# Trainium2 kernel: output projection, norm and feed-forward of each block in one stage, weights tile by tile, the norm's factor at the exits from PSUM

## The reference, cut to what matters

```python
def _rmsnorm(x, w):
    xf = x.astype(jnp.float32)
    y = xf * lax.rsqrt(jnp.mean(xf * xf, axis=-1, keepdims=True) + EPS)
    return (y * w.astype(jnp.float32)).astype(x.dtype)

def _conv_ffn(h, w_up, ffn_conv, ffn_conv_bias, w_down):
    gate, up = _split(h @ w_up, (D_FF, D_FF))
    gate = _dwconv(gate, ffn_conv) + ffn_conv_bias
    return (jax.nn.silu(gate) * up) @ w_down

for l in range(DEPTH):
    h = _rmsnorm(x, mix_norm[l])
    x = x + _mixer(h, ...)
    h = _rmsnorm(x, ffn_norm[l])
    x = x + _conv_ffn(h, w_up[l], ffn_conv[l], ffn_conv_bias[l], w_down[l])
...
```

## Time and profile before

| | |
|---|---|
| median of 3 runs | 3351.74 us (3351.55 to 3360.6) |
| profiled execution | 3355.1 us, its span 3353.2 us |
| mean granted TensorE clock | 0.962 |
| PE busy | 3059.8 us, 91% |
| PEld / DVE / ACT / POOL busy | 76% / 48% / 35% / 14% |
| DMA | 235 MB, 70 GB/s over the span |

### The profile page before, as it was taken

How to read it: one execution, slowest core, us unless ns; L and a number is a source line. 1 busy time by engine, 2 the same in 40 slices (tenths; PEclk the granted TensorE clock), 3 DMA queues, 4 the chain that set the end, 5 groups by cost and what they waited for, 6 DMA issues and landing times. The chain is left out here.

```text
span 3353.2 us, 40954 instructions
## 1 busy us (share of the span) xinstructions
PE 3059.8 (91%) x15744; PEld 2534.2 (76%) x15744; DVE 1617.2 (48%) x2106; ACT 1181.0 (35%) x1647; POOL 479.8 (14%) x279
## 2 busy tenths in 40 slices
PE   6899899886999989898998978999898999969899
PEld 5799888775887867898887856887676767758787
DVE  4566547533554345565476334553475552233233
ACT  3543543323222234334543232222333652232222
POOL 2332003001000022330030000000162223110000
PEclk9999999998999999999999988999999999989999
DMA  4100300322222231002103222222431222223122
GB/s 148 51 1 1 100 26 20 101 76 78 87 92 72 92 102 49 26 1 75 50 1 101 76 75 88 92 83 82 122 82 49 71 63 79 66 75 98 65 95 93
DMA packets 264333, 235.11 MB, mean 70 GB/s; under 512 B 23188, under 2 KB 247938, under 8 KB 263554
## 3 DMA queue, kind: packets, MB, share of 16 engines
q1 hardware_dynamic: 264194, 233.20, 23.0%
HBM read 226.88 MB, written 6.29 MB: 70 GB/s over the span
## 5 line engine op out<-in xcount | busy, mean ns | idle before, releaser
L120 PE MATMUL PS<-HHI,WHI 128*128 128x512 f32 x2016 | 805.4, 399 | 93.3 <-DVE WLO L172 70.5
L121 PE MATMUL PS<-HLO,WHI 128*128 128x512 f32 x2016 | 797.2, 395 | 0.0
L122 PE MATMUL PS<-HHI,WLO 128*128 128x512 f32 x2016 | 796.6, 395 | 0.0
L172 DVE TENSOR_TENSOR WLO<-RAW,WHI 128x1024 fp32r<-128x1024 f32 (+2 forms) x212 | 361.6, 1707 | 513.8 <-ACT WHI L168 512.7
L168 ACT CAST WHI<-RAW 128x1024 fp32r<-128x1024 f32 (+2 forms) x212 | 304.1, 1437 | 744.3 <-PE PS L122 611.8
L120 PEld LDWEIGHTS PS<-HHI,WHI 128*128 128x128 f32 x2016 | 382.7, 190 | 194.1 <-issue 78.5
L122 PEld LDWEIGHTS PS<-HHI,WLO 128*128 128x128 f32 x2016 | 382.2, 190 | 87.8
L121 PEld LDWEIGHTS PS<-HLO,WHI 128*128 128x128 f32 x2016 | 382.9, 190 | 86.7 <-issue 2.0
L120 PE MATMUL PS<-SH,WHI 128*128 128x512 f32 x800 | 316.9, 396 | 45.1 <-DVE SL L379 45.1
L121 PE MATMUL PS<-SL,WHI 128*128 128x512 f32 x800 | 315.5, 394 | 0.0
L122 PE MATMUL PS<-SH,WLO 128*128 128x512 f32 x800 | 315.5, 394 | 0.0
(11 more groups left out here) (427 smaller groups left out, 4490.6 us busy)
## 6 DMA issues: line engine op xcount, KB each, us to landing
RAW<-in_w_up SPq DMA_DIRECT2D x44, 1024.0 KB, 5.1
RAW<-in_w_in SPq DMA_DIRECT2D x82, 512.0 KB, 4.1
RAW<-in_w_down SPq DMA_DIRECT2D x44, 512.0 KB, 3.3
RAW<-in_w_in SPq DMA_DIRECT2D x20, 1024.0 KB, 5.4
RAW<-in_w_gate SPq DMA_DIRECT2D x32, 512.0 KB, 4.0
RAW<-in_w_mlp SPq DMA_DIRECT2D x16, 1024.0 KB, 5.4
RAW<-in_w_mlp SPq DMA_DIRECT2D x32, 512.0 KB, 3.5
RAW<-in_w_out SPq DMA_DIRECT2D x24, 512.0 KB, 3.5
```

The lines of the kernel that those rows point to most:

```text
L120: e.matmul(out, wh, xh, start=first and n == 0, stop=False)
L121: e.matmul(out, wh, xl, start=False, stop=False)
L122: last = e.matmul(out, wl, xh, start=False, stop=final and n == len(quads) - 1)
L172: self.lo_st.done(dve.tensor_tensor(self.lo[:, s], self.raw[:, s], self.hi[:, s], ALU.subtract), f"unit{s}")
```

## The change

For each of the three blocks the four stages output projection, norm, up projection and down projection become one, `out_and_ffn_stage` (line 1482 of the changed kernel), written out without loops. `rms_stage`, `slab_stage`, `ffn_up_stage`, `mlp_up_stage` and `store_stage` are gone.

- **Weights.** All three projections take weights by output tile: 128 columns of 8 contraction tiles (11 or 8 for the down projection), in rows of 512 bytes. There are four slots instead of two. ACT casts each unit; POOL subtracts each but the first.
- **Output projection.** Per output tile 24 matmuls into one of four banks, then DVE adds it to X (line 1728) and makes XL (line 1713), ACT makes XH = X * weight (line 1673) and the square (line 1676), and PE sums the square two tiles later (line 1593).
- **Norm.** XH and XL hold X times the norm's weight without the factor RS. RS is made by ACT from the sum (lines 1679, 1681), and DVE applies it at the exit from PSUM.
- **Up projection.** The first three tiles are taken together, contraction tile by contraction tile. In a layer DVE does per hidden tile: times RS (line 1740), three taps (1744, 1747), the low part of the hidden tile before (1718), times the up tile (1752), times RS again (1754). ACT does silu (1691) and the high part (1697). In the MLP DVE does relu times RS in one instruction, ACT the square and the high part, DVE the low part.
- **Down projection.** The hidden tiles come in two groups; each group's down projection follows its up projection at once and is added to X. So hidden tiles are kept split, for one group only, in the buffers of M (8 tiles) and of `more`.
- **The stages before.** `branch_stage` and `attention_gate_stage` split M themselves (ACT cast, DVE subtract, one tile later) and load the first two units of w_out.
- **Output.** The transposes of tile m-1 follow tile m of the last down projection; ACT copies them out and SP stores.

```diff
 def branch_stage(...)
+                for r in range(2):
+                    feed.lo_st.wait(sp, T - 1, f"unit{r}")
+                    sp.dma_start(feed.raw[:, r, 0:8, :], k_tiles(w_out)[:, :, r * P:(r + 1) * P]).then_inc(tiles_in[r], 16)
...
+                def mixed_high(t):
+                    act.wait_ge(merged_s, t + 1)
+                    act.copy(MH[:, t, :], M[:, t % 2, :]).then_inc(mh_s, 1)
...
+                def mixed_low(t):
+                    dve.wait_ge(mh_s, t + 1)
+                    dve.tensor_tensor(ML[:, t, :], M[:, t % 2, :], MH[:, t, :], ALU.subtract).then_inc(ml_s, 1)
...
+def out_and_ffn_stage(nc, PS, C, X, mixed, raw01, in01, w_out, norm, w_up, w_down, conv, HID, wide_k, new, out=None):
+    K, N, R3 = X.shape[1], 4, range(3)
+    groups = [range(g * n_hid // 2, (g + 1) * n_hid // 2) for g in range(2)]
+    raw23 = new("RAW", [P, 2, wide_k, P])
+    WHI, WLO = new("WHI", [P, N, wide_k, P], F32R), new("WLO", [P, N, wide_k, P], F32R)
+    XH, XL = split_pair(new)
+    MH, ML = mixed
+    GP, ACC = new("GP", [P, 2, 514]) if conv is not None else None, new("ACC", [P, 2, 512])
...
+            def _(pe):
+                for t in range(K):
+                    low_ready(pe, t)
+                    if t >= 4:
+                        after(pe, dv, f"add{t - 4}")
+                    pt.done(product(pe, PS[:, 3 + t % 4, :], [(*weights(t, k), MH[:, k, :], ML[:, k, :]) for k in range(K)]), f"a{t}")
+                    if t >= 2:
+                        squares(t - 2)
+                for k in range(K):
+                    if k >= K - 1:
+                        squares(K - 2)
+                        squares(K - 1)
+                    after(pe, dv, f"xlo{k}")
+                    for n, tile in enumerate(tiles_in[0:3]):
+                        u = K + n
+                        if k == 0:
+                            low_ready(pe, u)
+                        last = product(pe, tile_bank(tile), [(*weights(u, k), XH[:, k, :], XL[:, k, :])], first=k == 0, final=k == K - 1)
...
+                        if final and m == 0:
+                            after(pe, dv, f"hlo{hidden[-1]}")
+                        elif m == 0:
+                            after(pe, dv, f"hlo{k0 + units[u][0] - 1}")
...
+            def _(act):
+                def high(u):
+                    act.wait_ge(raw_in[u % N], landed[u])
+                    if u >= N:
+                        after(act, pt, jobs[u - N])
+                    ac.done(act.copy(slot(WHI, u), source(u)), f"hi{u}")
...
+                            dv.done(dve.tensor_tensor(gp[:, 1:513], tile_bank((i, 0)), RS[:, :], ALU.mult), f"g{i}")
...
+                            dv.done(dve.tensor_tensor(acc, acc, tile_bank((i, 1)), ALU.mult), f"h{i}")
+                            own(f"h{i}")
+                            dv.done(dve.tensor_tensor(acc, acc, RS[:, :], ALU.mult), f"hr{i}")
...
+            def _(pool):
+                for u in range(1, U):
+                    after(pool, ac, f"hi{u}")
+                    pool.tensor_tensor(slot(WLO, u), source(u), slot(WHI, u), ALU.subtract).then_inc(lo_s, 1)
```

More of the change, by code:

```diff
@@ L262, in _ @@
                     dve.tensor_copy(PAR[:, n:n + m, :].rearrange("p a n -> p (a n)"), PS[:, n // 4, 0:m * P]).then_inc(rows_kept, 1)
[L265 to L319, removed]
@@ L322, in k_tiles @@
 def k_tiles(w):
     return w.rearrange("(k p) n -> p k n", p=P)
[L327 to L399, removed]
-                    if not final:
-                        used.done(last, f"slab{s}")
-                use(0, 0, True, False)
-                use(0, 1, False, False)
-                with pe.Fori(1, K // 2 - 1) as g:
-                    for s in range(2):
-                        use(g, s, False, False)
-                use(K // 2 - 1, 0, False, False)
-                use(K // 2 - 1, 1, False, True)
@@ L1624, in _ @@
             def _(sp):
-                early.load_first(sp)
-                with sp.Fori(1, T) as g:
+                for u in range(2, U):
+                    if u >= N:
+                        low_ready(sp, u - N)
+                    sp.dma_start(source(u), units[u][1]).then_inc(raw_in[u % N], 16)
+                if out is not None:
+                    for m in range(K):
+                        after(sp, ac, f"row{m}")
+                        dst = out.rearrange("(c p) f -> p c f", p=P)[:, :, m * P:(m + 1) * P]
+                        sp.dma_start(dst, ROWS[:, :, m % 2, :]).then_inc(stored[m % 2], 16)
@@ L1627, in _, with weights @@
                     for s in range(2):
[L1628 to L1629 removed]
+                        sp.wait_ge(stored[s], 16 * K // 2)
             @block.tensor
             def _(pe):
[L1633 to L1640 removed]
+                def weights(u, k):
+                    return WHI[:, u % N, k, :], WLO[:, u % N, k, :]
@@ L1672, in _ @@
-                turns(dve, T, body)
-            @block.scalar
-            def _(act):
-                silu.open(act)
-                feed.hi_st.open(act)
-                feed.split_hi(act, 0, 0)
-                feed.split_hi(act, 0, 1)
-                def body(g, more):
-                    for m in range(2):
-                        dve_st.wait(act, g, f"tap2_{m}")
-                        silu.done(act.activation(tile(HID, g * 2 + m), ACC[:, m, :], ACT.Silu), f"tile{m}")
-                        if more:
-                            feed.split_hi(act, g + 1, m)
-                turns(act, T, body)
+                own = lambda name: after(dve, dv, name)
@@ new lines, in _ @@
+                if conv is not None:
+                    dve.memset(GP[:, :, 0:1], 0.0)
+                    dv.done(dve.memset(GP[:, :, 513:514], 0.0), "pad")
+                after(dve, ac, "hi0")
+                dv.done(dve.tensor_tensor(slot(WLO, 0), source(0), slot(WHI, 0), ALU.subtract), "lo0")
+                for t in range(K):
+                    after(dve, pt, f"a{t}")
+                    dv.done(dve.tensor_tensor(X[:, t, :], X[:, t, :], PS[:, 3 + t % 4, :], ALU.add), f"add{t}")
+                    if t:
+                        x_low(t - 1)
```

451 lines of the change are left out of this document (263 added, 188 removed).

## The result

The changed kernel takes 3269.24 us in the median of four executions (3264.25 to 3274.13), the kernel before 3353.85 beside it: a ratio of 0.9745 (95% interval 0.9727 to 0.9763), 84.6 us less. The forecast was 3250 in a range of 3230 to 3290. The profiled execution took 3264.25, where the sum said 3253.2.

What follows compares the result with a forecast made beforehand. PE, busy 3059.8 of 3353.2 us, was taken as the bound, with gains only in its idle time and pace. Layers -63.0 and second block -38.9 made -101.9: 3253.2 profiled, 3250 median, range 3230 to 3290.

Steps and rivals of the forecast that it cites:

- Into the output projection: PE's idle gap before the output projection: 10.15 to 7.3 us, 2.9 gained per layer; 0.8 lost in the second block.
- The norm: Stretch of 34.4 us between output and up projection: only sums stay, 26.0 gained per layer, 26.7 in the second block.
- the stall behind the root: Early up projection: units cast after ACT's root come late, 1.5 us in a layer, 0.8 in the MLP.
- From up to down: PE waits 4.5 us (3.0 to 5.5) before each layer down projection, twice: 4.0 lost; the MLP's 8.90 goes.
- The slow starts: Half clock after PE idles: 2.5 us gained, 1.0 lost per layer; 2.5 and 1.0 gained in the second block.
- PE's pace: Layers' up projection: weights back on multiples of 128 bytes speed up 1056 matmuls, 7.0 us gained per layer.
- the middle, 1.9: M's buffers, 32 bytes short of a multiple, slow 576 matmuls per block: 1.9 us lost, bounds 0 and 3.9.
- The second block: Its terms, from the output projection to the program's end, sum to 38.9 us gained.
- The pace does not come back: Rival, 0.12: WHI's place is not the cause or misplaced M costs as much; 14 us stay out, 3264.
- The norm still stands in the way: Rival, 0.10: ACT and POOL hand over the first three units late, ten us a block, 3280.
- DVE and POOL block one another: Rival, 0.08: in the layers' up projection DVE takes 12.0 us per hidden tile, 1.1 above PE; 3298.
- POOL becomes the bound: Slower-than-before rival, 0.03: POOL's subtraction limits the stages once its mean passes 5.44 us; 3470 at 6.5.

Runs made afterwards that it cites:

- wait_root: Changed kernel, but PE sums the last two squares right behind the output projection and waits for the finished root before the up projection: 3286.82 us, ratio 0.9786.
- late_pool: Changed kernel, but POOL subtracts the two weight units beside a group's last hidden tile only after that tile's low part: 3256.73 us, one execution.
- whi_off: Changed kernel with WHI and WLO of the layers' joint stage moved up 32 bytes, off multiples of 128: 3278.75 us, ratio 0.9767.
- before_gp_pad: Kernel before with 96 bytes of padding behind ACC, so WHI and WLO begin at a multiple of 128 bytes: 3357.38 us, ratio 1.0005.
- m_aligned: Changed kernel with 96 bytes of padding ahead of M's right-hand buffers in each block: 3266.43 us, ratio 0.9725.
- late_wait: Changed kernel, but in each layer group's first down tile PE takes the eight older hidden tiles first, then waits for the three youngest singly: 3241.5 us, ratio 0.9653.

## Why the prediction was right, and where its terms were off

The sign, the mechanism and the size came out: 90.9 us less in the profiled execution against 101.9 in the sum. Of the 11.0 missing, 9.2 are the layers' stages and 1.8 the stages that the change does not touch.

- **Into the output projection.** 10.15 became 7.26 (7.3 forecast); in the second block 5.72 became 6.29 (0.8 lost forecast, 0.6 measured).
- **The norm.** 34.4 became the sums, 6.9; 26.0 forecast, 27.5 measured, since the stall behind the root (1.5) did not come: no two products of the up projection stand more than 0.25 us apart there but where sums lie between them. `wait_root` shows that this cover is worth 6 a block.
- **From up to down.** The term that failed in size: "3.0 to 5.5, I take 4.5" measured 6.15 and 6.13, outside the bounds. I had POOL disturb one instruction of the chain. It disturbs two places: the second tap, which makes the silu late (0.9 of the wait), and the low part (2.2). By the rule of the Trainium skill the prediction had 5.5, nearer, since it lets DVE wait for the whole subtraction; but it too was applied at one place. `late_pool` gives 3.04, the prediction's undisturbed 3.0. So 7.2 lost per layer in place of 4.0.
- **The slow starts.** -2.5 and +1.0 a layer, -1.5 in sum; measured -1.4 (before 2.0, 2.7 and 2.1; now 1.7, 2.4 and 1.4). That this came out is in part luck: behind the same wait of 6.1 us the slow start cost 1.4 to 3.0 in the traces of this study, 2.4 and 1.4 in the changed kernel, and nothing in the prediction tells the two apart. In the second block -3.5 was forecast and -4.3 measured.
- **PE's pace.** 7.0 per layer was the right size (`whi_off` takes 6.6 of it back), by a wrong cause: `before_gp_pad` put the weights on the multiples and gained nothing. The change brings WHI to the remainder of HHI by luck. With the right cause M's cost would have been known: its distance is 96, so it pays the whole 0.0067 a matmul, the upper bound of 3.9, not "the middle, 1.9"; `m_aligned` got it back.
- **The second block** gained 38.9, as forecast, in part by errors that cancel: with the measured sizes its sum is +0.6 - 27.5 - 4.3 - 8.9 + 3.9 - 2.5 = -38.7, where the norm and the slow starts gave more and M took more than forecast. PE had no wait before its last projections: the eight older tiles covered the chain, as the text said. The prediction did not ask why the layers' first down unit, which takes all 11 tiles, should not be split in the same way; `late_wait` does that.
- **The rivals.** *The pace does not come back* came true for M and not for the weights. *The norm still stands in the way* did not. *DVE and POOL block one another* was true of the durations (44 of 88 taps took 2.8 or 3.6 us against 0.75) and false of its consequence: in the steady state PE did not wait, it waited where nothing lay between DVE and PE. *POOL becomes the bound*: its mean is 2.6 us against the 5.44 that would decide.

With the measured sizes a layer's sum is -2.9 - 27.5 - 1.4 + 7.2 - 7.0 + 3.9 = -27.7, where -26.9 was measured; the last 0.8 is left open.

## What to carry to other kernels

When stages are joined, ask of each border what PE can do while the last piece of data is made, and let it wait for the pieces one by one, the youngest last: that was worth 16 us a layer, more than the whole shift of the norm's factor. Work that is moved to POOL is free on average and dear in a chain: look at each DVE instruction on the path, above all those with two inputs in SBUF, count each of them that can meet POOL, and bound each by its own length plus POOL's. And compare the pace of matmuls of the same form between stages; a 3% difference at the same granted clock was a matter of where buffers lie, and pads of under 256 bytes got it back.

## What the runs showed of the chip beyond that

- A 128x512 fp32r matmul stream runs at 0.2267 us from start to start when weights and moving data lie at the same remainder modulo 256 bytes in SBUF, and at 0.2333 at distances of 32, 64, 96 and 128, both at a granted clock of 1.00; the output projection's 0.2271 to 0.2293 in three runs are the exception. Other distances were not tried. The Trainium skill (TensorE: Matmul & The Clock Gate, Step-by-step: what each phase is for) has the loading of the next weights take no read bandwidth from the running matmul. No run here shows whether the weight load is what slows the stream; if it is, that sentence does not hold for every place of the buffers. Why the distance matters was only observed, not explained.
- Which of the two starts first decides who waits. In the changed kernel each DVE instruction with two SBUF inputs that starts beside a running POOL subtraction ends some 0.55 us after it: taps of 2.8 to 3.6 in place of 0.75, low parts of 0.8 to 2.9 in place of 0.69. A tap that was already running when POOL's began took its 0.75, and POOL's took 3.66 against 3.22. One form with a single SBUF input waited too: eight of 44 TENSOR_SCALAR (line 1744) started beside a subtraction and took 1.5 to 1.9 in place of 0.55.
- The half clock behind an idle time of PE did not go by the length of that time: 12 and 7 slow matmuls behind 6.15 and 6.13 us (changed kernel), 14 and 12 behind two of 6.13 (`m_aligned`), 9 and 14 behind two of 3.04 (`late_pool`), nine behind 2.82 (`wait_root`). In the joint stages a slow start cost 1.4 to 3.0 us.
